# Three 256-column products in one accumulator, taken out by ScalarE, in the stage hg of a two-block transformer kernel

## The reference

```python
h = rmsnorm(x, g_pre_mix[l]) * (1.0 + scale1) + shift1
proj = h @ w_in[l]
q_a, k_a, v_a, q_h, f_h, i_h, g_h, gate_a, gate_h = jnp.split(proj, splits, axis=-1)
...
f = lb + (1.0 - lb) * jax.nn.sigmoid(f_raw.astype(jnp.float32))
...
qc = chunks(jax.nn.silu(q.astype(jnp.float32)), HG_EXPAND)
kc = chunks(key, HG_EXPAND)
vc = chunks(i, HG_HEAD_V)
...
y_h = (o_h * jax.nn.sigmoid(g_h)) @ w_hgrn_proj[l]
```

## Time and profile before

| | us |
|---|---|
| median of 3 runs | 2606.26 |
| lowest and highest run | 2606.03, 2606.55 |
| the profiled execution | 2604.68 |
| its span in the profile | 2602.6 |
| PE, PEld, DVE, ACT busy in the span | 2528.3, 2220.3, 1833.1, 1305.6 |
| mean granted TensorE clock | 0.988 of full speed |
| moved by DMA | 550.69 MB, mean 212 GB/s |

### The profile page before, as it was taken

How to read it: one execution, slowest core, us unless ns; L and a number is a source line. 1 busy time by engine, 2 the same in 40 slices (tenths; PEclk the granted TensorE clock), 3 DMA queues, 4 the chain that set the end, 5 groups by cost and what they waited for, 6 DMA issues and landing times.

```text
span 2602.6 us, 41917 instructions
## 1 busy us (share of the span) xinstructions
PE 2528.3 (97%) x14936; PEld 2220.3 (85%) x14936; DVE 1833.1 (70%) x2266; ACT 1305.6 (50%) x1701; POOL 28.1 (1%) x32
## 2 busy tenths in 40 slices
PE   4899999999999999999999999999999999999999
PEld 4888888888887888888888877888888888888888
DVE  6789998787787555676555665566677774477774
ACT  1345556666446444444444445445555554455543
POOL 0000000000000000000000000030000000000000
PEclk9699999999999999999999999999999999999999
DMA  9899985555694666797666546654565556556665
GB/s 370 303 340 315 314 299 172 170 154 169 207 310 128 187 188 190 250 308 259 189 190 188 192 155 186 186 155 150 174 194 186 188 189 201 189 178 193 191 195 163
DMA packets 493559, 550.69 MB, mean 212 GB/s; under 512 B 18856, under 2 KB 450992, under 8 KB 493456
## 3 DMA queue, kind: packets, MB, share of 16 engines
q1 hardware_dynamic: 492032, 544.20, 64.4%
q0 software_dynamic: 1424, 5.13, 0.7%
HBM read 547.14 MB, written 2.11 MB: 211 GB/s over the span
## 4 chain that ended last, share of the span: by engine, by line
PE 79%; DVE 9%; issue 5%; ACT 3%; DMA 2%; SPq 1%; DVEq 0%; ACTq 0%
PE psg L1896 74%; PE pss L1896 4%; DVE w_lo L1216 2%; DVE gate_acc_mix L1203 2%; ACT w_hi L675 1%; DMA raw<-in_w_in 1%; DVE first_acc L1291 1%; SPq L545 1%; DMA stage<-in_w_ada 1%; DMA raw<-in_w_out 0%; DVE proj L1175 0%; DMA gate_w_mix<-in_w_ada 0%; ACT X L764 0%; DVE sq_mix L1647 0%; DVE X L1704 0%
## 5 line engine op out<-in xcount | busy, mean ns | idle before, releaser
L1896 PE MATMUL psg<-X,w_hi 128*128 128x512 f32 x4512 | 1577.6, 394 | 7.8 <-DVE proj L1175 3.3
L1216 DVE TENSOR_TENSOR w_lo<-raw,w_hi 128x1024 fp32r<-128x1024 f32 x832 | 1008.6, 1229 | 590.2 <-ACT w_hi L675 580.7
L675 ACT ACTIVATE w_hi<-raw 128x1024 fp32r<-128x1024 f32 x832 | 867.8, 1057 | 796.3 <-PE psg L1896 743.8
L1896 PE MATMUL psg<-X,w_lo 128*128 128x256 f32 x4512 | 1249.7, 282 | 0.0
L1896 PEld LDWEIGHTS psg<-X,w_hi 128*128 128x128 f32 x4512 | 841.9, 188 | 184.2 <-issue 9.2
L1896 PEld LDWEIGHTS psg<-X,w_lo 128*128 128x128 f32 x4512 | 854.5, 189 | 12.6 <-issue 1.4
L1896 PE MATMUL psg<-hid,w_hi 128*128 128x512 f32 x1664 | 575.8, 392 | 0.2 <-issue 0.2
L1896 PE MATMUL psg<-hid,w_lo 128*128 128x256 f32 x1664 | 458.5, 280 | 0.0
L1896 PEld LDWEIGHTS psg<-hid,w_hi 128*128 128x128 f32 x1664 | 309.8, 188 | 66.3 <-issue 0.6
L1896 PEld LDWEIGHTS psg<-hid,w_lo 128*128 128x128 f32 x1664 | 312.6, 188 | 3.3
L669 ACT ACTIVATE half<-psg 128x512 f32<-128x512 f32 x204 | 118.4, 580 | 3.3 <-PE psg L1896 3.3
(11 more groups left out here) (304 smaller groups left out, 1516.9 us busy)
## 6 DMA issues: line engine op xcount, KB each, us to landing
raw<-in_w_in SPq DMA_DIRECT2D x212, 512.0 KB, 4.3
raw<-in_w_ffn_in SPq DMA_DIRECT2D x176, 512.0 KB, 3.6
raw<-in_w_up SPq DMA_DIRECT2D x176, 512.0 KB, 4.8
raw<-in_w_ffn_out SPq DMA_DIRECT2D x88, 512.0 KB, 4.6
raw<-in_w_down SPq DMA_DIRECT2D x88, 512.0 KB, 4.5
gate_w_mix<-in_w_ada SPq DMA_DIRECT2D x160, 256.0 KB, 5.5
stage<-in_w_ada SPq DMA_DIRECT2D x64, 512.0 KB, 10.5
raw<-in_w_out SPq DMA_DIRECT2D x64, 512.0 KB, 4.4
```

Of the source, the lines that this page charges most:

```text
L675: nc.scalar.activation(w_hi[:, half_slot(j, p), :, :], raw[:, slot_of(j, p), :, :], ACT.Copy).then_inc(hi_ready, 1)
L1216: nc.vector.tensor_tensor(w_lo[:, hs, :, :], raw[:, slot_of(j, p), :, :], w_hi[:, hs, :, :].bitcast(F32), ALU.subtract).then_inc(raw_used, 1)
L1896: return nc.tensor.matmul(out_, l, r_, start=start, stop=stop)
```

## The change

In hg alone, a k-tile and column tile has three 256-column products into columns 0:S of its bank: `w_hi` by X's high half, `w_hi` by X's low half, `w_lo` by X's high half, in this order at the last k-tile too. The bank then holds the finished sum. ScalarE's `take_half` and VectorE's `take_sum` are dropped in hg. ScalarE takes each bank pair straight out of PSUM into `heads4` with the group's own function (Silu, sigmoid, copy, sigmoid) at the end of the group, and this raises `ps_free`. The functions of hg at p = 4, p = 8 and p = 0, and the one at p = 0 of m1, are gone. Waits on the old function counter `SH["act"]` become waits on `ps_free`, and the later jobs' `half_ready` targets are lowered by hg's 16.

```diff
@@ -421,6 +421,11 @@
+        def halves_done(j, i, g):
+
+            hg = J["hg"]
+            return group_no(j, i, g) + 1 - (hg.iters * len(hg.groups) if j.G0 > hg.G0 else 0)
+
         POOL_BANK = (1, 0, 3, 2)
@@ -694,6 +699,8 @@
                                                      ).then_inc(half_ready, 1)
+                        elif p in j.ends and j.name == "hg":
+                            after(i, j.ends[p])
                         elif p in j.ends:
@@ -868,20 +875,17 @@
-                def gate_function(i, g):
-                    act.wait_ge(ps_free, sums_done(J["hg"], i, g))
+                def out_of_bank(i, g):
+                    b = bank_of(J["hg"], g)
+                    act.wait_ge(pe_chunk, chunks_done(J["hg"], i, g))
+                    act.wait_ge(ps_free, sums_done(J["hg"], i, g) - 1)
                     apart()
-                    t = heads4[:, ds(2 * i, 2), g, :]
-                    nc.scalar.activation(t, t, ACT.Silu if g == 0 else ACT.Sigmoid).then_inc(SH["act"], 1)
+                    ins = nc.scalar.activation(heads4[:, ds(2 * i, 2), g, :], psg[:, b:b + 2, 0:CW],
+                                               (ACT.Silu, ACT.Sigmoid, ACT.Copy, ACT.Sigmoid)[g])
+                    ins.then_inc(ps_free, 1)
...
-                    if p == 0 and not is_first(b):
-                        gate_function(b - 1, 3)
-                    if p == 4:
-                        gate_function(b, 0)
-                    if p == 8:
-                        gate_function(b, 1)
                     if p == 9 and final:
@@ -914,13 +918,12 @@
-                job(J["hg"], None, side, None, True)
+                job(J["hg"], out_of_bank, side, None, True)
...
                     if is_first(i) and p == 0:
-                        gate_function(J["hg"].iters - 1, 3)
                         act.preload_act_table_set("natural_log_exp_and_others")
@@ -1171,7 +1174,7 @@
-                dve.wait_ge(half_ready, group_no(j, i, g) + 1)
+                dve.wait_ge(half_ready, halves_done(j, i, g))
                 nc.vector.tensor_tensor(dst, psg[:, b:b + 2, 0:CW], half[:, b // 2, :, :], ALU.add).then_inc(ps_free, 1)
@@ -1179,7 +1182,7 @@
                     d = x_res[:, 14 + t, :]
-                    dve.wait_ge(half_ready, group_no(j, j.iters - 1, g) + t + 1)
+                    dve.wait_ge(half_ready, halves_done(j, j.iters - 1, g) + t)
                     nc.vector.tensor_tensor(t_g[:, t, :], psg[:, b + t, 0:CW], half[:, b // 2, t, :], ALU.add
@@ -1243,7 +1246,7 @@
                             g = j.ends[p]
-                            if not early:
+                            if not early and j.name != "hg":
                                 take_sum(j, i, g, dest(i, g))
@@ -1447,7 +1450,7 @@
-                dve.wait_ge(SH["act"], 12)
+                dve.wait_ge(ps_free, sums_done(J["hg"], 3, 3))
                 dve.wait_ge(SH["rs"], h + 1)
@@ -1520,7 +1523,7 @@
-                        dve.wait_ge(SH["act"], 3 * i + 2)
+                        dve.wait_ge(ps_free, sums_done(J["hg"], i, 1))
                         for a in range(2):
@@ -1923,7 +1926,11 @@
                                 o = psg[:, b + t, :]
-                                if kk < kt - 1:
+                                if j.name == "hg":
+                                    mm(o[:, 0:S], hi, x[:, at, 0:S], kk == 0, False)
+                                    mm(o[:, 0:S], hi, x[:, at, S:2 * S], False, False)
+                                    ins = mm(o[:, 0:S], lo, x[:, at, 0:S], False, kk == kt - 1)
+                                elif kk < kt - 1:
                                     mm(o, hi, x[:, at, :], kk == 0, False)
```

## The result

| | us |
|---|---|
| before, median of 20 runs | 2606.27 |
| changed, median of 20 runs | 2611.0 |
| ratio | 1.0018, 95% interval 1.0012 to 1.0024 |
| changed, span of the profiled execution | 2609.6 |

The account below looks back on a forecast made before the run. TensorE (PE), busy 97% of the span, was taken to bound the kernel. Turn 0 0.5, turns 1 to 3 5.4, wait behind the stage -0.8: +5.1 us on the 2606.3 median, 2611.4 us; range 2604.5 to 2614.5.

Parts of the forecast that it names:

- The stream: PE in hg: each of 512 triples takes 6 ns more than a pair, 3.1 us before waits hide part.
- 0.24 + 0.2: PE's growth in us per turn in turns 1 to 3: chunks 5 to the scores, then chunks 12 to 15.
- the 113 ns: Weight loads in a row take 113 ns each, just under 117.5 ns per product, so three fit in a triple.
- The page's rule: Trainium skill: N / 2.4 GHz plus 2.5 ns per product; third products would add 1.3 us instead of 3.1.
- ScalarE's step 7: Table load and sigmoid precede w_hi at p = 7; `probs` about 1.35 us later in turns 1 to 3, 0.3 in turn 0.
- The wait behind the stage: PE's 0.9 us wait for `gate_acc_mix` just behind hg: 0.8 us of it goes.
- The waits in turn 0: Growth of 0.24 us disappears in the 0.9 us `qr` wait, chunks 5 to 11 in the 2.40 us `probs` wait.
- The freed VectorE wins: Rival: w_hi not held up at p = 7, `probs` comes earlier; -1.5 us, 2604.7 us; chance 0.10.
- Every product pays 13.4 ns: Rival: equal overhead per product in hg, chunks grow by 107 ns; +6.9 us, 2613.2 us; chance 0.15.
- the loads no longer hide: Rival: each triple's third weight load is exposed, 0.11 us each; 56 us, some 2662 us; chance 0.09.
- the third product is free: Rival: 0 ns per triple in hg; +3.8 us, 2610.1 us; chance 0.08.
- the doubled table switch: Rival: a switch right behind `es` takes 1.28 us more, delaying `probs` four times; 2616.5 us; chance 0.03.

Follow-up runs that it names:

- e1_late_exit: The changed kernel with the function of group 1 moved behind w_hi of step 8; 2601.56 us against 2605.94 for the kernel before, ratio 0.9982.
- e9_late_exit_pairs: e1_late_exit with the 512- and 256-column pairs of the kernel before instead of triples; 2600.08 us, 1.5 below e1_late_exit.
- e7_early_table: The kernel before with the sigmoid's table loaded at the end of step 7, ahead of w_hi of step 8; 2612.02 us against 2606.30, ratio 1.0023.
- e4_longer: The changed kernel with one more 1024-column ScalarE instruction per turn, ahead of w_hi of step 8; 2616.54 us, 5.5 above the changed kernel.
- e3_exit_only: The changed kernel with the pairs of the kernel before, keeping ScalarE's new order; 2608.81 us against 2605.94 for the kernel before, ratio 1.0011.

## Why the prediction was right

**The stream: right in kind, the term too large.** The step "three of them make 352.5 ns, 5.6 to 6 ns more than a pair" took the cost of two adjacent low products for all, and rounded up. It is close to the dearer of two levels (353 ns). The mean in the changed kernel is 350.5 ns, 3.3 more than a pair, and a turn shows the same: what isn't hidden in it, 72 triples, grew by 0.26 us (0.14 up to the scores and 0.12 from the transposes on, turn 1), 3.6 ns each, where the forecast had 0.24 + 0.2. Put into the forecast's own sum that is about 0.2 us less in each of turns 1 to 3, and the sum falls from 5.1 to some 4.6; 4.7 was measured. The loads hide, as the 113 ns said. The page's rule, put aside then, is nearer for this step: the Trainium skill (TensorE: Matmul & The Clock Gate, "Wait — 56ns, not 53.3ns?") has 2.5 ns for each product beside its columns. The runs show 2.8 and 6.1 at the two levels; and a pair takes 347.2 ns where an estimate by that rule gives 325, so it doesn't give the price of a whole product here.

**ScalarE's step 7: right.** From the scores to the transposes of turn 1 it is 240.98 to 263.48 before and 244.19 to 268.01 after, +1.32 us against the forecast's +1.35; in turn 0 +0.23 (24.37 to 24.60) against +0.3. VectorE's wait is 1.89 us, forecast 1.9. PE's wait is 1.69, forecast "about 1.5", and 2.48 in turn 0, "still above 2". Turns 1 and 2 grew by 1.58 and 1.51 us (from one rotation of the queries to the next), forecast 1.8; most of what lies between them is that 0.2 of the stream.

**The wait behind the stage: right.** 0.94 fell to 0.26; 0.8 was to go and 0.7 went.

**The waits in turn 0: wrong, and outweighed.** The stream's growth before the scores was to disappear in the wait for `qr`. The wait itself grew, from 0.87 to 1.49 us, and the way from the rotation to the scores from 13.91 to 14.67. It hangs on a transfer, as the forecast says: ScalarE's w_hi ahead of it waited 7.48 us for its landing, 6.76 before. In the ten kernels profiled here the wait was 0.3 to 1.5 us, so a single profile can't give its size.

**What the forecast left out: the clock.** The profiled execution of the changed kernel lost some 1.6 us to a fall of PE's clock in turn 0, and that of the kernel before as much behind the stage (last section). So turn 0 grew by 2.66 us, forecast 0.5, and the way from the last rotation to the first head shrank by 0.62, where the forecast had +1.0. The two cancel. That the profiles give 5.1 us for hg, the forecast's very figure, is luck to this extent: 0.8 too little before turn 0's scores, 0.5 too much for the stream, and two falls of the clock that nobody forecast. The mechanism and the waits of turns 1 to 3, which carry most of the loss, are not.

**The rivals.** "The freed VectorE wins" was put aside for the order of ScalarE's queue; e1_late_exit restores the order, and then it does win, with 2601.6 us where that rival had 2604.7. It is 3.1 us lower than worked out there. About 1.1 of it is the stream's smaller term (of that rival's 2.5 us of unhidden stream, 3.5 ns in place of 6 leaves 1.5); for the rest the clock, below, is the likely reason. "Every product pays 13.4 ns" and "the loads no longer hide" fall with 350 to 353 ns, "the third product is free" with e9_late_exit_pairs, and the doubled table switch with e7_early_table.

**Outside hg** nothing moved by over 1 us: from the first head of m1 to the first product of the job out (402.39 to 694.57 before, 407.93 to 700.86 after) it is 292.2 and 292.9 us, as forecast.

## What to carry to other kernels

A function taken straight out of a bank saves an instruction on each of two engines, but it stands where the copy stood: look at what is queued behind it, and count the table load as part of it. Move it behind the work on which the next engine hangs as soon as its bank has time; here one step later turned a loss of 4.7 us into a gain of 4.4. And work taken from an engine that is 95% busy in a stage gains nothing at a point where that engine itself waits for another: take one wait of the bound engine and follow its chain back through every queue before you price the relief.

## What the runs showed of the hardware

PE's granted clock fell to its lower level (1.2 of 2.4 GHz) for a little over 3 us behind some of these short waits, and not behind others of the same length. The stretches of 4 us that hold the falls, in the kernel before, in the changed one, and in e4_longer, two of its three (length; busy PE, PEld, DVE, ACT, POOL; clock; DMA share; GB/s):

```profile
396.00:400.00 4.00, 4.00 (x16) 3.42 (x16) 3.85 (x4) 3.96 (x5) 0.00 (x0) 0.57 0.51 153
```

```profile
212.00:216.00 4.00, 4.00 (x26) 4.00 (x24) 3.93 (x6) 0.00 (x0) 0.00 (x0) 0.61 0.68 204
```

```profile
270.00:274.00 4.00, 4.00 (x23) 4.00 (x22) 3.89 (x7) 0.00 (x0) 0.00 (x0) 0.57 0.67 200
382.00:386.00 4.00, 3.93 (x22) 3.93 (x23) 3.93 (x6) 0.89 (x2) 0.00 (x0) 0.61 0.65 184
```

In the kernel before it came behind the 0.94 us wait for the gates, in the changed one behind the 2.48 us before the transposes of turn 0. The same stretch showed no fall in e3_exit_only, whose wait there was 2.66 us, and e1_late_exit has none in hg or m1. A fall costs about 1.6 us: from the sums of the gates to the first head's transposes it took 8.14 us before, with a fall, and 6.58 after, without one. So a wait that is removed can be worth more than its length. In the profiled executions this accounts for what the waits leave over. From the rotation of turn 0 to the first head, e1_late_exit takes 8.95 us less than the changed kernel: 7.6 by all the waits and 1.6 by one fall less. e4_longer takes 6.3 more: 2.8 by the waits and 3.2 by two falls more. It is the likely reason for the 1.9 us by which the medians of both went past what was expected, in opposite directions; with one profile for each kernel that is argued, not shown.

Splitting a 512-column product in two with the same weights (three products of 256 columns in place of 512 and 256) costs 3.5 ns in the mean. The triples follow each other at one of two distances, 350.0 or 353.3 ns, for whole stretches of a turn, and neither the order of the weights nor the columns that they write decides which; pairs of 512 and 256 have 347.2 ns in all kernels that have them. Each product has its own weight load, also when its neighbour has the same weights (15448 of each in the changed kernel).
